# First attention of a two-block forward pass: the first shift from TensorE's matmuls to VectorE's dots, and another order of VectorE's work around the heads

## The chip, the cores and the metric

The kernel runs on one core of one Trainium2 chip. The metric is the device time of one execution in microseconds, as the median of several runs. One launch computes everything in float32. TensorE multiplies weights in two float32r parts each (a high part and the rest), with three matmuls for each product.

## The reference, cut to what matters

Two blocks are computed one after the other on 256 tokens of width 1024. The change touches the very first stage, the multi-head latent attention of layer 0 and what is computed ahead of it:

```
cond = silu(c)                                   # c: 1 x 1024
mod = cond @ ada_w[0] + ada_b[0]                 # 1 x 6144
sh1, sc1, g1, sh2, sc2, g2 = split(mod, 6)
h = rmsnorm(x, norm_g[0, 0]) * (1 + sc1) + sh1   # 256 x 1024
proj = h @ mla_w_in                              # 672 columns: 384 q, 256 kv, 32 rope
c_q, c_kv = rmsnorm(proj[:, :384]), rmsnorm(proj[:, 384:640])
q = c_q @ w_uq; kv = c_kv @ w_ukv                # 16 heads; rope on 32 columns of q and k
o = softmax(q k^T / sqrt(96) + chunk mask) v     # a head at a time
x = x + g1 * (o @ mla_w_out)
h = rmsnorm(x) * (1 + sc2) + sh2
x = x + g2 * (silu(h @ w_gate) * (h @ w_up)) @ w_down
...                                              # a Mamba layer with eight experts, then block two
```

## The kernel before

**Weights.** All weights of the program pass in one list of tiles, in the order in which they are loaded. SyncE loads a tile into the next of six slots of `raw` (`NRAW`) as soon as the tile that was there six places earlier has been used. A tile has one of three kinds.
- "w": ScalarE copies it into `parts` (the high part, `hi`, L245), VectorE subtracts that from it (the rest, `low`, L260), and its slot of `raw` is free after that. `parts` has five places (`NSPLIT`), so tile m's high part waits for the matmuls with tile m - 5. The text counts these tiles as m0, m1 and so on: m0 to m5 are `mla_w_in`, m6 to m17 the up projections of four groups of heads (m6 to m8 for group 0, m9 to m11, m12 to m14 and m15 to m17 for groups 1 to 3), m18 to m25 `mla_w_out`, m26 to m91 the first feed-forward layer in eleven steps (four tiles of gate and up, and two of down, each step), and m92 is the first of the Mamba layer.
- "dot": 128 rows of the transposed `ada_w`. VectorE multiplies it with the broadcast condition row `crow` and sums along the row (L625): 128 of the 6144 numbers of `mod` as a column in `acols`. After each fourth dot the bias is added (L631). `rows_pe` makes a row of four columns with four small matmuls (L292), broadcast over all partitions.
- "plain": TensorE takes it as it is, in float32. Only `Start` uses these.

**Start.** `Start.FIRST = (2, 3, 0, 1)` lists four blocks of 512 columns of `ada_w`: 2 and 3 are `sc1`, 0 and 1 are `sh1`. Each is four plain tiles, eight matmuls (16 instructions in the trace) and a bias matmul. `scale_dve` makes `mod` and the scaled `xn` of each half, and `shift_dve` adds the shift out of the banks. Then TensorE turns `xn` over in four pieces (`x_pieces`), ScalarE and VectorE split each into `hTh` and `hTl` (L414, L421), and the projection `in` begins (L286 to L288).

**Heads.** A slot h of the loop does, on TensorE, the scores of head h, the turning of head h - 1's probabilities and the values of head h - 2. VectorE takes the maximum of head h (L808, L809), the reciprocal of head h - 1 (L842) and the values of head h - 2 (L866). ScalarE does the exponentials (L817, L818). Four slots lie between one group's projections and the next. Among them stand the next group's `kv` and `q` projections, the rotation of its queries (`q_dve`, L1014 to L1029) and the copies of its keys (`kT_dve`, L1074). `K.W.low(v)` stands at written places in `Mla.dve`. It runs all dots that precede the next "w" tile in the list, and then that tile's split.

All orders are written out by hand; each engine runs its own list, and semaphores are waited for where a value comes from another engine. `Ffn.dve` is not changed by the diff: it calls `K.W.low(v, 4)`, then `hid_dve` (the product with silu and its split, L1448 and L1451, between ScalarE's L1439 and L1441), then `K.W.low(v, 2)`, for each step.

## Time and profile before

| what | value |
|---|---|
| median of 3 runs | 2807.74 us (2806.32 to 2808.96) |
| the profiled execution | 2809.04 us, of which 2807.2 us span |
| TensorE matmuls busy | 94% of the span |
| VectorE, ScalarE busy | 70%, 56% |
| DMA | 616.35 MB, mean 220 GB/s |
| granted clock of TensorE, mean | 0.966 |

The profile is of one execution, 1.3 us longer than the median of the runs. Times within it are microseconds from the start of its span. The attention of layer 0 with what precedes it fills about the first 213 us, the first feed-forward layer runs to about 422 us. "Busy" of TensorE says that a matmul was under way, whatever clock it ran at; the clock stands in a column of its own (1.00 is 2.4 GHz, 0.50 is 1.2 GHz).

### The profile page before, as it was taken

The numbers are of one execution on the slowest core, as the hardware profiler recorded it, in microseconds if no ns is written. First come the engines' busy times: TensorE is split into PE (matmuls) and PEld (weight loads), VectorE is DVE, ScalarE is ACT, GpSimd is POOL, SyncE is SP. The second block draws the span as 40 slices with busy tenths as digits, with TensorE's granted clock in tenths as the row PEclk, the third lists the DMA queues.
The fourth block names the chain that finished last, engine by engine and source line by source line (L and its number), as shares of the span: only waits on it lengthen the run. The fifth ranks groups of instructions, "written<-read, shape, count | busy, mean of one in ns | idle before, by whom it ended". The sixth has DMA issues, their size and how long they took to land.

```text
span 2807.2 us, 39117 instructions
## 1 busy us (share of the span) xinstructions
PE 2649.9 (94%) x15496; PEld 2304.3 (82%) x15496; DVE 1961.1 (70%) x2819; ACT 1565.7 (56%) x2266; POOL 10.9 (0%) x24
## 2 busy tenths in 40 slices
PE   7788998998999999999996999999999999999998
PEld 3677998886888888888885998887898998887898
DVE  3768887876898899889896556555555556655555
ACT  2443445653777777778775445465444445455444
POOL 0000000000000000000000000000000000000000
PEclk9889998998999999999997999999999999999999
DMA  8537984514899999999995665434565665434563
GB/s 276 188 119 261 352 311 127 174 48 133 298 365 342 334 350 350 332 344 366 335 354 189 194 185 175 141 98 128 173 188 151 202 185 176 147 97 130 164 186 115
DMA packets 349599, 616.35 MB, mean 220 GB/s; under 512 B 20705, under 2 KB 174881, under 8 KB 349409
## 3 DMA queue, kind: packets, MB, share of 16 engines
q1 hardware_dynamic: 346402, 603.35, 64.6%
q0 software_dynamic: 1872, 5.99, 0.7%
q10 hardware_dynamic: 1136, 4.44, 0.4%
q8 instruction: 125, 2.05, 0.3%
q14 instruction: 64, 0.52, 0.1%
HBM read 612.66 MB, written 1.05 MB: 219 GB/s over the span
## 4 chain that ended last, share of the span: by engine, by line
PE 84%; DVE 8%; ACT 4%; DMA 2%; issue 1%; DVEq 0%; ACTq 0%
PE pb L286 24%; PE pb L288 24%; PE pb L287 24%; PE pb L292 8%; DVE parts L260 2%; PE pb L408 2%; ACT parts L245 1%; DMA raw<-in_moe_w_up 1%; PE pb L2215 1%; PE pb L2671 1%; DVE raw L625 1%; DMA X<-in_x 0%; DVE hTl L421 0%; ACT pb L478 0%; DVE xn L509 0%
## 5 line engine op out<-in xcount | busy, mean ns | idle before, releaser
L260 DVE TENSOR_TENSOR parts<-raw,parts 128x1024 fp32r<-128x1024 f32 (+2 forms) x1051 | 1265.2, 1216 | 590.6 <-ACT parts L245 556.2
L245 ACT ACTIVATE parts<-raw 128x1024 fp32r<-128x1024 f32 (+2 forms) x1051 | 1103.1, 1054 | 824.6 <-PE pb L288 699.7
L286 PE MATMUL pb<-parts,arenar 128*128 128x512 f32 (+2 forms) x1696 | 667.9, 394 | 14.7 <-DVE arenar L421 6.1
L287 PE MATMUL pb<-parts,arenar 128*128 128x512 f32 (+2 forms) x1696 | 649.5, 383 | 0.0
L288 PE MATMUL pb<-parts,arenar 128*128 128x512 f32 (+2 forms) x1696 | 648.7, 382 | 0.0
L286 PE MATMUL pb<-hTh,parts 128*128 128x256 f32 x1952 | 559.5, 287 | 7.3 <-DVE hTl L421 4.9
L287 PE MATMUL pb<-hTl,parts 128*128 128x256 f32 x1952 | 558.3, 286 | 0.0
L288 PE MATMUL pb<-hTh,parts 128*128 128x256 f32 x1952 | 557.9, 286 | 0.0
L286 PEld LDWEIGHTS pb<-hTh,parts 128*128 128x128 f32 x1952 | 381.0, 195 | 11.9 <-issue 7.1
L286 PEld LDWEIGHTS pb<-parts,arenar 128*128 128x128 f32 x1696 | 321.4, 190 | 80.5 <-issue 16.3
L287 PEld LDWEIGHTS pb<-hTl,parts 128*128 128x128 f32 x1952 | 380.9, 195 | 1.8
L288 PEld LDWEIGHTS pb<-hTh,parts 128*128 128x128 f32 x1952 | 380.7, 195 | 0.0
L288 PEld LDWEIGHTS pb<-parts,arenar 128*128 128x128 f32 x1696 | 321.0, 189 | 62.8
L287 PEld LDWEIGHTS pb<-parts,arenar 128*128 128x128 f32 x1696 | 321.5, 190 | 61.3 <-issue 5.6
L286 PE MATMUL pb<-parts,hTh 128*128 128x512 f32 (+3 forms) x560 | 224.2, 400 | 10.9 <-DVE hTl L421 8.4
L288 PE MATMUL pb<-parts,hTl 128*128 128x512 f32 (+3 forms) x560 | 216.5, 387 | 0.0
L287 PE MATMUL pb<-parts,hTh 128*128 128x512 f32 (+3 forms) x560 | 216.2, 386 | 0.0
L286 PEld LDWEIGHTS pb<-parts,hTh 128*128 128x128 f32 x560 | 108.4, 194 | 32.5 <-issue 10.6
L292 PE MATMUL pb<-arena 64*128 64x128 f32 (+6 forms) x696 | 129.6, 319 | 4.7 <-DVE arena L2139 2.6
L288 PEld LDWEIGHTS pb<-parts,hTl 128*128 128x128 f32 x560 | 108.3, 193 | 21.5
L287 PEld LDWEIGHTS pb<-parts,hTh 128*128 128x128 f32 x560 | 108.5, 194 | 17.8
L292 PEld LDWEIGHTS pb<-arena 64*128 64x128 f32 (+3 forms) x696 | 92.6, 195 | 26.1 <-issue 11.8
(287 smaller groups left out, 1969.4 us busy)
## 6 DMA issues: line engine op xcount, KB each, us to landing
raw<-in_moe_w_gate SPq DMA_DIRECT2D x176, 512.0 KB, 5.2
raw<-in_moe_w_up SPq DMA_DIRECT2D x176, 512.0 KB, 5.3
raw<-in_moe_w_down SPq DMA_DIRECT2D x176, 512.0 KB, 5.3
raw<-in_ffn_wg SPq DMA_DIRECT2D x88, 512.0 KB, 4.3
raw<-in_ffn_wu SPq DMA_DIRECT2D x88, 512.0 KB, 3.7
raw<-in_ffn_wd SPq DMA_DIRECT2D x88, 512.0 KB, 4.4
raw<-in_ada_wT SPq DMA_DIRECT2D x80, 512.0 KB, 5.2
raw<-in_w_in SPq DMA_DIRECT2D x72, 512.0 KB, 3.7
```

The lines of the kernel that those rows point to most:

```text
L245: a.e.activation(self.part(t, 0), self.slot(t), ACT.Copy).then_inc(*a.up(self.c.hi, t.m))
L260: v.e.tensor_tensor(self.part(t, 1), self.slot(t), self.part(t, 0).bitcast(F32), ALU.subtract).then_inc(*v.up(self.c.lo, t.m))
L286: e.matmul(o, a[0], b[0], start=start, stop=False, skip_group_check=True)
L287: e.matmul(o, a[0], b[1], start=False, stop=False, skip_group_check=True)
L288: return e.matmul(o, a[1], b[0], start=False, stop=stop, skip_group_check=True)
L292: return e.matmul(o, a, b, start=start, stop=stop, skip_group_check=True)
L408: m = t.e.transpose(b.t[0:w, j * P:(j + 1) * P], s, self.C["ident"])
L625: v.e.scalar_tensor_tensor(out=w, in0=w, scalar=1.0, in1=self.crow, op0=ALU.mult, op1=ALU.mult, accum_out=self.acols[:, o:o + 1]).then_inc ...
L2215: m = t.e.transpose(b.t[:, k * P:(k + 1) * P], self.hc[:, i % 2, k * P:(k + 1) * P], self.K.C["ident"])
L2671: m = t.e.matmul(b.t[:, 0:2 * NCMP], loads[k // 8][:, k % 8, :], self.flat[:, a, k, :], start=k == 0, stop=k == 15)
```

## The change

Six things are edited; all else is as it was.
- `FIRST` is `(2, 3)`. The shift's two blocks are no longer matmuls of plain tiles but eight dot tiles, `dot_tiles(0)` and `dot_tiles(1)`. Four of them stand among the scale's eight plain tiles (two plain, one dot, and so on), four behind. TensorE makes the rows out of the columns with four small matmuls each.
- `scale_dve` takes one half at a time, and dots stand ahead of each half and behind both.
- `low` counts "w" tiles and dots apart (`n_lo`, `n_dot`), and `dots` can be called alone.
- A slot of a head takes the maximum and the reciprocal first, then `low` (the dots and the split), then the values. `q_dve` and `kT_dve` stand behind the third slot instead of ahead of it.
- Within group 0, the rope of the keys and the turning of `krT` stand ahead of `q_dve` and `kv_pe`. Both pieces of `c` are turned before `q_pe`. No dot stands there but one. ScalarE's high parts of m9 to m13 are made together or later.
- The table of dots ahead of each tile is spread from m4 on instead of m4 to m7 and m13 on.

```diff
     def low(self, v, times=1):
-        while times and self.n_low < len(self.tiles):
-            t = self.tiles[self.n_low]
-            self.n_low += 1
-            if t.kind == "dot":
-                v.wait_ge(*self.landed(t))
-                self.dot(v, t, self.slot(t))
-            if t.kind != "w":
-                continue
-            times -= 1
+        for t in self.cut[self.n_lo:self.n_lo + times]:
+            while self.n_dot < len(self.dotted) and self.dotted[self.n_dot].n < t.n:
+                self.dots(v)
+            assert all(x.n > t.n - self.nraw for x in self.dotted[self.n_dot:]), t.label
             self.n_lo += 1
...
+    def dots(self, v, times=1):
+        for t in self.dotted[self.n_dot:self.n_dot + times]:
+            self.n_dot += 1
+            v.wait_ge(*self.landed(t))
+            self.dot(v, t, self.slot(t))
...
-    FIRST = (2, 3, 0, 1)
+    FIRST = (2, 3)
...
+        scale = [Tile(("ada", n, k0), w[:, k0:k0 + 2, n * 512:n * 512 + 512], (2, 512), "plain")
+                 for n in self.FIRST for k0 in (0, 2, 4, 6)]
+        shift = self.K.dot_tiles(0)
+        mixed = sum(([*scale[2 * i:2 * i + 2], shift[i]] for i in range(4)), [])
+        return mixed + self.K.dot_tiles(1)
...
+        for n in range(2):
+            b = K.c.bk[4 + n]
+            t.wait_ge(*K.c.dv.val(("col", n)))
+            t.wait_ge(*b.turn(("ada", n)))
+            for j in range(4):
+                m = mm1(t.e, b.t[:, j * P:(j + 1) * P], K.acols[:, 4 * n + j:4 * n + j + 1].to_broadcast([P, P]),
+                        K.C["ident"])
+            m.then_inc(*t.up(K.c.pe, ("ada", n)))
...
-        dots = {4: 1, 5: 1, 6: 1, 7: 1, 22: 1, 23: 1} | {m: 2 for m in range(13, 22)}
+        dots = {m: 1 for m in (4, 5, 6, 7, 8, 9, 10, 12, 13, 14)} | {m: 2 for m in range(15, 22)}
...
     def slot_dve(self, v, h, lows=0):
         if h < 16:
             self.att.max_dve(v, h)
         if 1 <= h <= 16:
             self.att.sums_dve(v, h - 1)
+        self.K.W.low(v, lows)
         if h >= 2:
             self.att.values_dve(v, h - 2)
...
         self.c_pe(t, 0)
+        self.c_pe(t, 4)
         self.q_pe(t, 0)
-        self.c_pe(t, 4)
-        self.kv_pe(t, 0)
-        b = c.bk[6]
         t.wait_ge(*c.dv.val("kr"))
         K.turn_pe(t, "krT", 6, [self.kr[:, tt, :] for tt in range(2)])
+        self.kv_pe(t, 0)
...
         for j in range(2):
             self.qT_act(a, 0, j)
+        K.W.hi(a, 4)
...
-        self.start.scale_dve(v)
+        K.W.dots(v, 2)
+        self.start.scale_dve(v, 0)
+        K.W.dots(v, 2)
+        self.start.scale_dve(v, 1)
+        K.W.dots(v, 4)
+        K.W.low(v)
         self.start.shift_dve(v)
-        K.W.low(v, NSPLIT - 2)
-        for key, b, tt, k0, hi, lo in self.x_pieces():
+        for i, (key, b, tt, k0, hi, lo) in enumerate(self.x_pieces()):
             K.parts_dve(v, key, b, hi, lo)
+            if i % 2:
+                K.W.low(v)
...
         for g in range(1, 4):
             h = 4 * g - 4
-            K.W.low(v)
-            self.slot_dve(v, h)
-            K.W.low(v)
-            self.slot_dve(v, h + 1)
-            K.W.low(v)
+            for s in range(3):
+                self.slot_dve(v, h + s, 1)
             self.q_dve(v, g)
             for j in range(2):
                 self.kT_dve(v, g, j)
-            self.slot_dve(v, h + 2)
             self.slot_dve(v, h + 3)
```

On VectorE, at the start of the program, ahead of the first split pieces of `hT`, the order before was this (the `scale` operations write `mod` and `xn`, the `shift` operations read a bank `pb`):

```order
L744 SCALAR_TENSOR_TENSOR mod<-pb,grow 128x512 [waits s_matmul_done]
L748 SCALAR_TENSOR_TENSOR xn<-X,small,mod 128x512 [waits s_bank7_out]
L748 SCALAR_TENSOR_TENSOR xn<-X,small,mod 128x512
L762 TENSOR_TENSOR xn<-xn,pb 128x512 [waits s_matmul_done,s_vector_done]
L762 TENSOR_TENSOR xn<-xn,pb 128x512 [waits s_vector_done]
L762 TENSOR_TENSOR xn<-xn,pb 128x512 [waits s_matmul_done]
L762 TENSOR_TENSOR xn<-xn,pb 128x512 [waits s_vector_done]
L260 TENSOR_TENSOR parts<-raw,parts 128x1024 [waits s_weight_hi] x3
L421 TENSOR_TENSOR hTl<-pb,hTh 128x4x128 [waits s_scalar_done] x4
```

The change has this at the same place, from the second half of the scale on:

```order
L758 SCALAR_TENSOR_TENSOR mod<-pb,grow 128x512 [waits s_matmul_done]
L762 SCALAR_TENSOR_TENSOR xn<-X,small,mod 128x512 [waits s_bank7_out]
L762 SCALAR_TENSOR_TENSOR xn<-X,small,mod 128x512
L628 SCALAR_TENSOR_TENSOR raw,small<-raw,arena 128x1024 [waits s_raw0_landed]
L628 SCALAR_TENSOR_TENSOR raw,small<-raw,arena 128x1024 [waits s_raw1_landed]
L628 SCALAR_TENSOR_TENSOR raw,small<-raw,arena 128x1024 [waits s_raw2_landed]
L628 SCALAR_TENSOR_TENSOR raw,small<-raw,arena 128x1024 [waits s_raw3_landed]
L634 TENSOR_TENSOR small<-small 128x4 [waits s_vector_done]
L256 TENSOR_TENSOR parts<-raw,parts 128x1024 [waits s_weight_hi]
L776 TENSOR_TENSOR xn<-xn,pb 128x512 [waits s_matmul_done,s_weight_lo]
L776 TENSOR_TENSOR xn<-xn,pb 128x512 [waits s_vector_done]
L776 TENSOR_TENSOR xn<-xn,pb 128x512 [waits s_matmul_done]
```

Four dots and one split have come between the scale and the shift, and two of the three splits that stood ahead of the pieces of `hT` have gone among them. Four more dots stand further up.

On VectorE, around the third slot of the second group of heads, the order before was this (dots L625, split L260, then `q_dve` and `kT_dve`, then the slot's maximum):

```order
L625 SCALAR_TENSOR_TENSOR raw,small<-raw,arena 128x1024 [waits s_raw3_landed]
L625 SCALAR_TENSOR_TENSOR raw,small<-raw,arena 128x1024 [waits s_raw4_landed]
L260 TENSOR_TENSOR parts<-raw,parts 128x1024 [waits s_weight_hi]
L1014 TENSOR_SCALAR arena<-pb,small 128x384 [waits s_matmul_done] x2
...
L1074 COPY arena<-pb 64x512 [waits s_matmul_done] x2
L808 TENSOR_REDUCE small<-pb 128x1 [waits s_matmul_done]
L809 TENSOR_REDUCE small<-pb 128x1
L842 RECIPROCAL small<-small 128x2 [waits s_bank6_out,s_bank4_out]
L866 TENSOR_SCALAR arena<-pb,small 128x64 [waits s_vector_done,s_matmul_done]
```

The change has there:

```order
L822 TENSOR_REDUCE small<-pb 128x1 [waits s_matmul_done]
L823 TENSOR_REDUCE small<-pb 128x1
L856 RECIPROCAL small<-small 128x2 [waits s_bank6_out,s_bank4_out]
L628 SCALAR_TENSOR_TENSOR raw,small<-raw,arena 128x1024 [waits s_raw2_landed]
L628 SCALAR_TENSOR_TENSOR raw,small<-raw,arena 128x1024 [waits s_raw3_landed]
L256 TENSOR_TENSOR parts<-raw,parts 128x1024 [waits s_weight_hi]
L880 TENSOR_SCALAR arena<-pb,small 128x64 [waits s_weight_lo,s_matmul_done]
L880 TENSOR_SCALAR arena<-pb,small 128x64
L1028 TENSOR_SCALAR arena<-pb,small 128x384 x2
```

The maximum and the reciprocal of the third slot now precede the dots, the split and `q_dve`.

On VectorE, at the end of the first feed-forward layer's normalisation (the last two pieces of `hT`, then the splits of its weights, then dots), before:

```order
L421 TENSOR_TENSOR hTl<-pb,hTh 128x4x128 [waits s_scalar_done]
L260 TENSOR_TENSOR parts<-raw,parts 128x1024 [waits s_weight_hi] x3
L625 SCALAR_TENSOR_TENSOR raw,small<-raw,arena 128x1024 [waits s_raw4_landed]
L625 SCALAR_TENSOR_TENSOR raw,small<-raw,arena 128x1024 [waits s_raw5_landed]
L625 SCALAR_TENSOR_TENSOR raw,small<-raw,arena 128x1024 [waits s_raw0_landed]
```

and now:

```order
L424 TENSOR_TENSOR hTl<-pb,hTh 128x4x128 [waits s_scalar_done]
L256 TENSOR_TENSOR parts<-raw,parts 128x1024 [waits s_weight_hi] x4
L628 SCALAR_TENSOR_TENSOR raw,small<-raw,arena 128x1024 [waits s_raw4_landed]
L628 SCALAR_TENSOR_TENSOR raw,small<-raw,arena 128x1024 [waits s_raw5_landed]
L628 SCALAR_TENSOR_TENSOR raw,small<-raw,arena 128x1024 [waits s_raw0_landed]
```

The calls of `low` in the attention split 27 tiles before and split 26 now, so VectorE makes one split more here, and stays one tile further back in the list, against its other work, until the experts' last steps. ScalarE's high parts are as far along as they were.

## Rows read from the trace of the kernel before

**Rows 1.** The page: busy us, share of the span and instructions of each engine.
```profile
PE 2649.9 (94%) x15496; PEld 2304.3 (82%) x15496; DVE 1961.1 (70%) x2819; ACT 1565.7 (56%) x2266; POOL 10.9 (0%) x24
```

**Rows 2.** Stretches: us, busy PE, PEld, DVE, ACT, POOL; clock, DMA share, GB/s.
```profile
25.60:50.00 24.40, 24.40 (x56) 9.78 (x55) 5.59 (x8) 3.17 (x3) 0.00 (x0) 1.00 0.80 258
56.30:61.20 4.90, 4.85 (x12) 3.82 (x13) 4.90 (x7) 0.00 (x0) 0.00 (x0) 0.50 0.68 192
61.20:75.00 13.80, 13.80 (x86) 12.31 (x85) 7.46 (x13) 4.83 (x13) 0.00 (x0) 0.99 0.81 278
79.40:85.40 6.00, 6.00 (x20) 5.91 (x20) 2.23 (x12) 2.75 (x7) 0.00 (x0) 0.51 0.32 125
114.80:120.70 5.90, 0.01 (x2) 0.01 (x1) 5.66 (x18) 0.91 (x4) 0.00 (x0) 0.60 0.66 237
```

**Rows 3.** Timeline of TensorE: start, us, operation, count, [idle before, and its releaser].
```profile
33.74 7.13 PE L292 MATMUL pb<-raw,small 128*128 128x512 f32 x16
...
56.35 0.77 PE L286 MATMUL pb<-parts,hTh 128*128 128x512 f32 x1 [4.15 <-DVE hTl L421]
...
79.39 0.66 PE L286 MATMUL pb<-parts,arenar 128*128 128x384 f32 x1 [3.32 <-DVE arenar L421]
...
97.21 0.66 PE L408 MATMUL pb<-cst,small 128*96 128x128 f32 x2 [4.23 <-DVE small L1346]
97.66 3.62 PE L408 MATMUL pb<-cst,arena 128*96 128x128 f32 x16
...
128.08 0.83 PE L292 MATMUL pb<-arena 96*128 96x128 f32 x6
...
151.92 0.83 PE L292 MATMUL pb<-arena 96*128 96x128 f32 x6
...
173.17 1.48 PE L292 MATMUL pb<-arena 96*128 96x128 f32 x6
```

**Rows 4.** Timeline of VectorE up to the first weights.
```profile
23.48 0.18 DVE L1332 TENSOR_SCALAR small<-small 128x32 f32<-128x32 f32 x1
...
50.08 1.41 DVE L762 TENSOR_TENSOR xn<-xn,pb 128x512 f32<-128x512 f32 x2 [6.64 <-PE pb L292]
51.41 3.49 DVE L260 TENSOR_TENSOR parts<-raw,parts 128x1024 fp32r<-128x1024 f32 x3
54.81 2.47 DVE L421 TENSOR_TENSOR hTl<-pb,hTh 128x512 fp32r<-128x512 f32 x4
...
58.34 1.21 DVE L625 SCALAR_TENSOR_TENSOR raw<-raw,arena 128x1024 f32<-128x1024 f32 x1
```

**Rows 5.** DMA of 0 to 60 us: GB/s in 40 slices; loads, median to landing.
```profile
GB/s 0 172 204 362 401 394 355 133 268 393 411 407 400 412 388 350 270 350 247 190 220 272 300 335 137 292 224 221 298 299 213 188 337 330 294 75 301 179 282 45
...
raw<-in_ada_w SPq DMA_DIRECT2D x16, 512.0 KB, 4.7
```

**Rows 6.** Timeline of VectorE between the projection and the heads of group 1.
```profile
97.91 2.29 DVE L1268 COPY arena<-pb 32x2048 f32<-32x2048 f32 x1 [0.75 <-PE pb L408]
...
101.32 0.68 DVE L1074 COPY arena<-pb 64x512 f32<-64x512 f32 x1 [0.17 <-PE pb L408]
...
138.94 1.13 DVE L1014 TENSOR_SCALAR arena<-pb,small 128x384 f32<-128x384 f32 x2
```

**Rows 7.** Waits between 100 and 175 us: total us, times, longest.
```profile
PE pb L408 <- ACT arena L818: 19.0, 6, 6.2
```

**Rows 8.** The first feed-forward layer and the Mamba layer's start: a stretch, and timelines.
```profile
300.00:350.00 50.00, 50.00 (x354) 47.13 (x354) 43.88 (x64) 23.28 (x32) 0.00 (x0) 1.00 0.96 349
...
198.49 1.23 DVE L260 TENSOR_TENSOR parts<-raw,parts 128x1024 fp32r<-128x1024 f32 x1
...
225.75 3.49 DVE L260 TENSOR_TENSOR parts<-raw,parts 128x1024 fp32r<-128x1024 f32 x3
...
280.38 0.42 DVE L1448 TENSOR_TENSOR arena<-arena,pb 128x256 f32<-128x256 f32 x1
...
440.82 0.55 PE L286 MATMUL pb<-hTh,parts 128*128 128x256 f32 x1 [1.72 <-DVE hTl L421]
```

More of the change, by code:

```diff
@@ L199, in __init__ @@
         self.cut = [t for t in tiles if t.kind == "w"]
+        self.dotted = [t for t in tiles if t.kind == "dot"]
         self.place = {t.label: n for n, t in enumerate(tiles)}
@@ L677, in tiles @@
         w = wview(self.K.A["ada_w"][0])
-        return [Tile(("ada", n, k0), w[:, k0:k0 + 2, n * 512:n * 512 + 512], (2, 512), "plain")
-                for n in self.FIRST for k0 in (0, 2, 4, 6)]
+        scale = [Tile(("ada", n, k0), w[:, k0:k0 + 2, n * 512:n * 512 + 512], (2, 512), "plain")
[3 more added lines that the diff above has]
+        return mixed + self.K.dot_tiles(1)
     def sp(self, s):
@@ L735, in dve, with scale_dve @@
             K.stats_dve(v, "n0", tt)
[L737 removed]
+    def scale_dve(self, v, h):
         K, c, dv = self.K, self.K.c, self.K.c.dv
         v.wait_ge(*K.row_landed(0))
[L741 to L749 removed]
+        b, cs = c.bk[6 + h], slice(h * 512, (h + 1) * 512)
+        v.wait_ge(*c.pe.val(("ada", 2 + h)))
+        v.e.scalar_tensor_tensor(out=K.mod[:, 1, cs], in0=b.t[:, :], scalar=1.0, in1=K.row(0)[:, cs], op0=ALU.add,
+                                 op1=ALU.mult).then_inc(*v.up(b.out, ("ada", 2 + h)))
+        v.wait_ge(*v.tail)
+        for tt in range(2):
+            v.e.scalar_tensor_tensor(out=K.xn[:, tt, cs], in0=K.X[:, tt, cs], scalar=K.rst[:, tt:tt + 1],
+                                     in1=K.mod[:, 1, cs], op0=ALU.mult, op1=ALU.mult).then_inc(*v.up(dv))
     def shift_dve(self, v):
@@ L1236, in act @@
             self.slot_act(a, h + 2)
+            K.W.hi(a)
             self.slot_act(a, h + 3)
@@ L1256, in dve @@
         self.in_dve(v, 0)
-        K.W.low(v, 2)
+        self.in_dve(v, 1)
+        K.W.dots(v)
         self.c_dve(v, 0)
-        self.in_dve(v, 1)
+        self.c_dve(v, 4)
         self.roots_dve(v)
-        K.W.low(v, 2)
-        self.c_dve(v, 4)
+        self.key_rope_dve(v)
         self.q_dve(v, 0)
-        K.W.low(v)
-        self.key_rope_dve(v)
         b = c.bk[6]
```

24 lines of the change are left out of this document (6 added, 18 removed).

## The prediction

> **What bounds the kernel now.** I read the page first: TensorE is busy 94% of the span, VectorE 70% [rows 1]. That mean hides the stage which is changed. Its stretches come next [rows 2]. From 25.6 to 50 us TensorE is busy without a pause, while VectorE has 5.6 us of work in 24.4. From 114.8 to 120.7 it is the other way round: VectorE 5.7 of 5.9 us, TensorE 0.01. So the scale and shift matmuls bound the first 50 us, and VectorE bounds much of the head loop. TensorE's timeline [rows 3] shows where it stands before a dependent start: 4.15 us before the projection at 56.35 (for `hTl`), 3.32 us before the queries at 79.39, 4.23 us before the key turning at 97.21. In the head loop it waits 19.0 us in six waits for exponentials [rows 7]. These are not late for ScalarE's sake but because the maximum ahead of them is queued behind VectorE's dots, split and `q_dve`.
>
> All that follows the attention starts from its end, so a shift there passes through to the end of the program, less what VectorE's new place in the weight list costs later.
>
> **1. The front, up to the projection.** A block of plain matmuls takes 7.13 us and its bias about 1 us [rows 3]; two go, 16 us. In their place stand eight dots of 1.14 us each (1.21 in the row, which overlaps its neighbour) [rows 4]: 9.2 us. The loads stay 16 tiles of 512 KB ahead of m0. Nothing moves faster than about 400 GB/s, 1.3 us a tile, and a tile lands 4.7 us after its issue [rows 5]. I walk the new list with these.
> - The first six loads do not wait, as before, and block 2 ends at 25.6. VectorE is free at 23.7 [rows 4]: dots 0 and 1 end at 24.8 and 26.0. The third dot's load and all behind it now wait for dot 0, and land at about 29, 30.4, 31.7 and 33. Block 3 has two plain tiles of these and ends at 35 instead of 33.8.
> - The second half of the scale (2.1 us) ends at 37.3. The last four dots, landed by 38.3, end at 41.9, and the column's bias at 42.1. Split m0 ends at 43.3 (the tile lands at about 39.4, where the list before had it at 44.5). The shift, twice 1.4 us, ends at 46.1, and the first two pieces of `hTl` at 47.4.
>
> The projection starts at 47.4 instead of 56.35: **-8.9**. Before, from the shift's end at 51.5 three splits (3.4 us) preceded the pieces [rows 4]; now one does, and one is hidden among them. If the loads came no faster than at the 258 GB/s of that stretch [rows 2], m2 would land 3 to 4 us later and ScalarE's pieces, queued behind its high part, with it: -5.
>
> **2. From the projection to the first keys.** It took 45.6 us from 56.35 to the second key copy's end at 102.0 [rows 3, 6]. Now: the projection runs 18.6 us as before, to 66.0, cold at its start as before. `in_dve(1)` and one dot end at 67.9, the two turned pieces of `c` at 69.2 and 69.6. The queries' matmuls start at 69.2 (3.3 us behind the projection instead of 4.4) and take 6 us at half clock. The roots and key rope, 4.2 us, run on VectorE beside them, where before they came later and behind two splits and two dots. So `krT` and `kv` follow at once: TensorE reaches 80.1, turns queries and keys (3.6 us [rows 3]) to 83.8; the copy of 2.29 us [rows 6] and split m9 lie beside that, and the second key copy ends at 84.5. That is 37.1 us: **-8.5**. What was skipped must now be made before the first maximum: `low(3)` is two dots and three splits, 4.9 us, where two dots and a short split stood, 3.9 us. Further, ScalarE's high part of m13 waits for a tile loaded into a slot that a dot frees at 85.6, and ends at 90, just when the maximum is ready; the table load of the exponential is hidden in it. I take **+1.0** for both, bounds 0 and +4 (a load at 4.7 us and one load queued ahead of it).
>
> **3. The head loop.** Dots fall from six to four in the first group: two times 1.14, of which the walk keeps **-1.6** at the next group's first scores (head 4, ending at 110.9 instead of 128.9 [rows 3], with all terms so far). For the second group I add VectorE's work from scores to rope: maximum, reciprocal, two dots, split, values are 4.3, 4.0 and 4.6 us, two waits of 0.5 for scores, and 2.8 for `q_dve` (138.94 on, [rows 6]). Then follow on TensorE 1.8 us of turning, 4.0 of the next `kv` at partly half clock and 1.0 of scores: 23.5 against 23.8 before (to 152.75). The third group gives 21.4 against 21.9 (to 174.65 [rows 3]). So **-0.8** for both. The stall is moved, not removed: the exponential no longer waits behind `q_dve`, but `q_dve` and with it the next group's queries wait behind the third slot's dots and split. The tail from head 12 on is TensorE's and stays.
>
> Attention: -8.9 - 8.5 + 1.0 - 1.6 - 0.8 = **-18.8**.
>
> **4. The clock, a gain not in the sum above.** From 79.4 to 85.4 TensorE ran at 0.51 after 3.32 us idle [rows 2, 3]. Now it idles some 2 us there. If it stays at full speed, 3 us of 6 go, of which the rope lets 2.8 through. Taken at a quarter: **-0.7**. The Trainium skill (TensorE: Matmul & The Clock Gate, What's actually happening) has the clock follow recent activity, full after sustained work and half after idleness. By it the bursts between waits stay half-speed, and the term would be 0; the rows show both levels, 0.50 at 56.3 and 0.99 from 61.2.
>
> **5. VectorE one tile further back.** One fewer `low` in the attention has three prices.
> - The feed-forward layer's first tile was split at 198.49, under TensorE's matmuls; three splits stood ahead of the dots at 225.75 [rows 8]. Now four do, and one slot of six stays filled, so one more load of 1.3 us lies between there and m30, for which TensorE waits at 240: **+1.3**.
> - In each step `hid_dve` moves ahead of a dot and a split. VectorE stands for a silu which ScalarE makes behind the next tile's high part: 2 tiles of 1.3 us, 0.4 for silu, less the split of 1.2, 1.8 us a step. A step is 120 matmuls, 354 take 50 us, so 16.95 us [rows 8]. VectorE is busy 43.88 of 50 us, 14.9 a step, 15.2 with the gaps in `hid_dve` (280.38 to 282.87). With the new wait it needs 17.0 to 17.1, just above TensorE. Besides, the slots of two tiles come free some 4 us later, with DMA busy 0.96 of the stretch; the round of load, high part and silu grows by up to 1.1 us. Bounds: 0 (TensorE stays the bound) and 1.1 over nine steps, 10. I take 0.4: **+3.5**. By the Trainium skill (DMA: Bandwidth & Descriptors, Where 436 GB/s comes from) some 358 GB/s is what memory gives a core; the row's 349 is close, and by that rule a hole is not made up, which is the upper bound.
> - The Mamba layer's first tile was split ahead, and TensorE began at 440.82 when `hTl` was there [rows 8]. Now the split comes between: **+0.8**. Some **+0.4** for two or three places in Mamba and the experts, by the same shift; bounds 0 and 1.5.
>
> **The sum.** -18.8 - 0.7 + 1.3 + 3.5 + 0.8 + 0.4 = -13.5. It is made against the profiled execution, 2809.04 to 2795.5; that one lies 1.3 over the median, so the median goes from 2807.74 to **2794.2**.
>
> **Rivals.**
> - *A. As summed*, with the feed-forward stage giving back a third: -9 to -17, 2791 to 2799. Chance 0.50.
> - *B. TensorE stays the bound of the feed-forward steps*, and the clock helps. For it speaks that TensorE is busy 50.00 of 50, and a tile's lead there may take 2 us. Then -18.8 - 2.1 + 1.3 + 0.8 + 0.4 = -18.4: 2789 (2784 to 2791). Chance 0.20.
> - *C. The later silu bites fully*, 1.1 in nine steps, or the head groups lose what they win since `q_dve` waits behind 3.4 us of dots and split, 2 us a group. DMA share 0.96 speaks for the first, VectorE's 5.66 of 5.9 for the second. -13.5 + 6 = -7.5: 2800 (2799 to 2802). Chance 0.18.
> - *D. The front gives little*: the interleaved loads wait for VectorE, and 0.8 of DMA is busy [rows 2] already. Front -4 instead of -8.9, and some of C: -4, 2804. Chance 0.07; it is "no change" when under 5.6 us.
> - *E. Slower.* One mechanism: the silu wait in the feed-forward layer also idles DMA, so each of eleven steps grows. It decides from 18 / 11 = 1.6 us a step on, half of a split and dot more than I can find; at 2.5 us it gives -17 + 27 = +10, 2818. Against it: two splits and two dots' worth of wait a step would have to be paid in full. Chance 0.05.
>
> 0.2% is 5.6 us, about what a measurement of this kernel can tell from no change. Faster: A, B, C and none of D, 0.88. Same 0.07, slower 0.05. The range 2787 to 2802 takes A, C and half of B.
>
> **What would show it.** In the trace after: the projection's first matmul at 47 to 48; the second key copy ending at 82 to 85; scores of head 4 near 111, of head 8 near 134.5, of head 12 near 156; four splits in a row 18 to 20 us earlier than 225.75; steps of the feed-forward layer at 17.0 (B), 17.3 (A) or 18 us (C); TensorE's start in Mamba 0.8 us behind `hTl`. I am wrong if the third dot's load is later than 26, if `krT` still waits for the key rope, or if high part m13 holds the first exponential beyond 93.

## The result and the profile after

| | median us | lowest to highest | runs |
|---|---|---|---|
| before | 2805.99 | 2801.73 to 2808.97 | 10 |
| after | 2812.74 | 2808.86 to 2820.73 | 10 |

The ratio is 1.0031, with a 95% interval of 1.0020 to 1.0043: the change makes the kernel slower by 0.3%, where 0.5% faster was forecast. The profiled execution of after, 2808.86 us with a span of 2807.1, is the fastest of its ten, and that of before, 2809.04 us, is longer than any of its ten, so the two traces show less of the difference than the medians do.

The page after, in the form of [rows 1], shows hardly anything:

```profile
PE 2637.7 (94%) x15476; PEld 2300.9 (82%) x15476; DVE 1963.3 (70%) x2837; ACT 1565.1 (56%) x2266; POOL 10.9 (0%) x24
```

What tells is when TensorE first uses a weight tile. This table is read from the traces of before, of after, and of two experiments below (e1: after, with VectorE's missing split made up at the attention's end; e2: before, with that split taken out). Shifts are against before, in us.

| tile | before at | after | e1 | e2 |
|---|---|---|---|---|
| m0, projection | 56.35 | -8.95 | -8.76 | +0.08 |
| m1 | 61.50 | -11.18 | -10.98 | -0.15 |
| m9, keys of group 1 | 101.29 | -20.29 | -20.41 | -0.31 |
| m18, output projection | 181.18 | -20.74 | -20.47 | -0.42 |
| m25, its last | 207.39 | -20.74 | -20.46 | -0.41 |
| m26, feed-forward layer | 224.70 | -18.42 | -20.46 | +1.91 |
| m50 | 300.06 | -12.55 | -21.02 | +7.52 |
| m86, its last step | 401.94 | -1.24 | -20.84 | +19.39 |
| m92, Mamba layer | 440.82 | +3.14 | -18.28 | +23.57 |
| m550, late in the experts | 1311.86 | +3.98 | -22.16 | +25.67 |

The attention won 20.7 us, and by m92 all of it was given back: 2.3 us at m26, 17.2 from there to m86, 3.4 from m86 to m88 and 1.0 at m92. The first part lies at TensorE's start in the layer. The wait for VectorE at m26, then at m30, was this before:

```profile
224.70 0.55 PE L286 MATMUL pb<-hTh,parts 128*128 128x256 f32 x1 [0.22 <-DVE hTl L421]
...
240.00 0.39 PE L286 MATMUL pb<-hTh,parts 128*128 128x256 f32 x1 [1.83 <-DVE parts L260]
```

and is this after, where m26's own split is late and m30's less so:

```profile
206.28 0.58 PE L289 MATMUL pb<-hTh,parts 128*128 128x256 f32 x1 [2.54 <-DVE parts L256]
...
221.12 0.39 PE L289 MATMUL pb<-hTh,parts 128*128 128x256 f32 x1 [0.81 <-DVE parts L256]
```

The 3.4 us between m86 and m88 are 0.9 us of wait and 2.5 us of clock in the 48 matmuls of the rows. These three lines are of before, of after and of e1; the granted clock over them was 1.00, 0.64 and 0.63:

```profile
410.66 5.97 PE L292 MATMUL pb<-cst,small 128*128 128x128 f32 x48 [2.80 <-DVE arena L1448]
```

```profile
410.31 8.44 PE L295 MATMUL pb<-cst,small 128*128 128x128 f32 x48 [3.69 <-DVE arena L1464]
```

```profile
389.82 8.54 PE L295 MATMUL pb<-cst,small 128*128 128x128 f32 x48 [2.80 <-DVE arena L1464]
```

e1 has no lag and the wait of before, and its trace lost the 2.5 us as well, so they don't come of the lag.

**The attention after.** TensorE's timeline (start, us, operation, count, idle before and its releaser), at the places of [rows 3]:

```profile
68.57 0.66 PE L289 MATMUL pb<-parts,arenar 128*128 128x384 f32 x1 [2.47 <-DVE arenar L424]
...
73.85 0.42 PE L411 MATMUL pb<-cst,small 128*96 128x128 f32 x2 [0.54 <-DVE small L1362]
...
106.96 0.83 PE L295 MATMUL pb<-arena 96*128 96x128 f32 x6
...
130.25 0.83 PE L295 MATMUL pb<-arena 96*128 96x128 f32 x6
...
152.37 1.48 PE L295 MATMUL pb<-arena 96*128 96x128 f32 x6
```

The key turning at 73.85 waits 0.54 us for the rope, where it waited 4.23. Heads 4, 8 and 12 are scored 21.1, 21.7 and 20.8 us sooner than in [rows 3]. VectorE's two key copies, in the form of [rows 6], and the wait of [rows 7], 20 us sooner (80 to 155 us), which was 19.0 us in six:

```profile
80.17 1.28 DVE L1088 COPY arena<-pb 64x512 f32<-64x512 f32 x2
```

```profile
PE pb L411 <- DVE arena L1043: 4.8, 3, 1.9
PE pb L295 <- DVE arena L880: 4.7, 5, 2.7
PE pb L411 <- ACT arena L832: 4.2, 2, 2.6
```

The stall is in good part moved. TensorE is spared 14.8 us of waits for exponentials (L832), and waits 9.5 us for the rotated queries (L1043) and for VectorE's values (L880).

**The feed-forward layer after.** The same stretch as in [rows 8] (us, busy PE, PEld, DVE, ACT, POOL; clock, DMA share, GB/s), and the waits in it (total us, times, longest):

```profile
300.00:350.00 50.00, 45.89 (x332) 43.23 (x331) 39.53 (x58) 21.11 (x29) 0.00 (x0) 1.00 0.85 304
```

```profile
DVE arena L1464 <- ACT arena L1455: 5.0, 3, 1.9
...
PE pb L289 <- DVE parts L256: 4.1, 3, 1.9
```

TensorE, busy for all of 50 us before, now waits 4.1 us, each time for a split. VectorE is idle too: in each step it waits for the silu. Nobody is the bound of this stretch by busy time. One round through SyncE (SPq), ScalarE, VectorE and TensorE, step m54 to m59 and the next, reads:

```profile
301.08 0.42 DVE L1464 TENSOR_TENSOR arena<-arena,pb 128x256 f32<-128x256 f32 x1 [1.56 <-ACT arena L1455]
...
303.57 1.22 DVE L628 SCALAR_TENSOR_TENSOR raw<-raw,arena 128x1024 f32<-128x1024 f32 x1
...
304.71 1.22 DVE L256 TENSOR_TENSOR parts<-raw,parts 128x1024 fp32r<-128x1024 f32 x1
...
309.27 2.36 DVE L256 TENSOR_TENSOR parts<-raw,parts 128x1024 fp32r<-128x1024 f32 x2
...
320.27 0.42 DVE L1464 TENSOR_TENSOR arena<-arena,pb 128x256 f32<-128x256 f32 x1 [1.53 <-ACT arena L1455]
```

```profile
311.66 0.38 SPq L237 DMA_DIRECT2D raw<-in_ffn_w_up  x1
```

```profile
318.91 1.06 ACT L246 ACTIVATE parts<-raw 128x1024 fp32r<-128x1024 f32 x1 [1.43 <-DMA raw<-in_ffn_w_up]
319.87 0.37 ACT L1455 ACTIVATE arena<-pb 128x256 f32<-128x256 f32 x1
```

```profile
305.99 0.39 PE L289 MATMUL pb<-hTh,parts 128*128 128x256 f32 x1 [1.25 <-DVE parts L256]
325.18 0.39 PE L289 MATMUL pb<-hTh,parts 128*128 128x256 f32 x1 [1.95 <-DVE parts L256]
```

From `hid_dve` to `hid_dve` it is a closed loop: `hid_dve` 2.49 us (301.08 to 303.57); dots and splits until m59's split frees a slot of `raw`, 8.06 (303.57 to 311.63); the load of the up tile m62 is issued 0.03 later, at 311.66, and its high part can begin 7.25 us later; 0.96 more until the silu, which ScalarE's list has behind that high part; 0.40 until `hid_dve`. The sum, 19.19 us, is the distance of the two TensorE starts (325.18 - 305.99 = 19.19). While VectorE stands for the silu and makes `hid_dve` it frees no slot, and the loads run dry. DMA of 300 to 320 us, in 40 slices of 0.5 us:

```profile
GB/s 381 395 408 457 418 410 328 205 41 0 0 106 131 311 410 197 188 311 303 246 274 350 344 367 360 350 373 379 432 393 381 375 389 412 444 399 369 383 418 428
```

### The profile page after: what moved, and what is told of

Its sections match the earlier page's. It is cut to its first block, busy times and chain, and to the rows that moved or that the text cites. A ratio compares the mean times of both kernels' runs of the same rounds, so it can differ in the third digit from the quotient of the medians.

```text
span 2807.1 us, 39082 instructions
## 1 busy us (share of the span) xinstructions
PE 2637.7 (94%) x15476; PEld 2300.9 (82%) x15476; DVE 1963.3 (70%) x2837; ACT 1565.1 (56%) x2266; POOL 10.9 (0%) x24
## 4 chain that ended last, share of the span: by engine, by line
PE 73%; DVE 13%; DMA 7%; ACT 5%; issue 2%; DVEq 0%; ACTq 0%
PE pb L289 21%; PE pb L291 21%; PE pb L290 21%; PE pb L295 8%; DVE parts L256 5%; DMA raw<-in_moe_w_gate 2%; DVE raw L628 2%; DMA raw<-in_ffn_w_up 2%; PE pb L411 2%; ACT parts L246 2%; DMA raw<-in_moe_w_up 1%; PE pb L2687 1%; PE pb L2231 1%; DMA X<-in_x 0%; DVE hTl L424 0%
## 5 line engine op out<-in xcount | busy, mean ns | idle before, releaser
L289 PE MATMUL pb<-hTh,parts 128*128 128x256 f32 x1952 | 561.4, 288 | 20.2 <-DVE parts L256 17.2
L290 PEld LDWEIGHTS pb<-parts,hTh 128*128 128x128 f32 x560 | 107.1, 191 | 17.5
```

What stands on the lines that cost most here:

```text
L289: e.matmul(o, a[0], b[0], start=start, stop=False, skip_group_check=True)
L290: e.matmul(o, a[0], b[1], start=False, stop=False, skip_group_check=True)
```

## The experiments

Times are compared through the ratio to the kernel before, run on the same chip.

| | edit | median us | ratio | 95% interval | step m50 to m86 |
|---|---|---|---|---|---|
| before | | | | | 16.98 |
| after | | 2812.74 | 1.0031 | 1.0020 to 1.0043 | 18.87 |
| e1 | after, lag made up | 2783.24 | 0.9929 | 0.9912 to 0.9946 | 17.01 |
| e2 | before, lag alone | 2833.16 | 1.0101 | 1.0085 to 1.0116 | 18.96 |
| e3 | after, ScalarE back too | 2784.88 | 0.9925 | 0.9905 to 0.9945 | 17.18 |
| e4 | after, short dots | 2804.22 | 1.0000 | 0.9988 to 1.0012 | 17.86 |
| e5 | after, short loads | 2793.00 | 0.9969 | 0.9959 to 0.9979 | 16.98 |
| e6 | after, silu sooner | 2791.37 | 0.9966 | 0.9954 to 0.9979 | 16.98 |
| e7 | e1, heads as before | 2783.55 | 0.9934 | 0.9922 to 0.9946 | 16.98 |
| e8 | after, keys as before | 2794.98 | 0.9973 | 0.9963 to 0.9982 | 16.98 |
| e9 | e1, silu and `hid_dve` sooner | 2781.68 | 0.9920 | 0.9907 to 0.9933 | 17.15 |
| e10 | e9, heads as before | 2783.90 | 0.9928 | 0.9914 to 0.9941 | 16.98 |
| e11 | e9, in both such layers | 2782.53 | 0.9920 | 0.9902 to 0.9938 | 17.05 |
| e12 | e6, lag made up later | 2787.18 | 0.9937 | 0.9922 to 0.9951 | 16.98 |

The last column is the distance of TensorE's starts of m50 and m86, over six steps.

### e1 and e2: the lag, away and alone

```diff
 # e1, on after, Mla.dve
             self.O_dve(v, tt, 4)
-        K.W.low(v)
+        K.W.low(v, 2)
         K.rows_dve(v, 0, 0, 2, (5, 6))
 # e2, on before, the same place
             self.O_dve(v, tt, 4)
-        K.W.low(v)
         K.rows_dve(v, 0, 0, 2, (5, 6))
```

> The changed kernel with one split more on VectorE at the attention's end (it makes m26 and m27 there, so that from the feed-forward layer on VectorE stands where it stood before the change). Theory L (the lag): all that the attention won, 20.7 us at the first tile of the output projection, was given back in the feed-forward layer because hid_dve had moved one tile forward against the splits; then the steps fall back to 16.98 us, and the time is 18 to 22 us under that of before, about 2786 us. Rival T (the time itself): the feed-forward layer starts 20 us earlier and meets the DMA queue in another phase, so that its steps lengthen whatever VectorE's place; then the steps stay at 18.5 to 19 us and the time stays within 5 us of that of the changed kernel, about 2810 us.

> The kernel before with the split at the attention's end taken out: nothing of the change but its lag of one tile. Theory L: the attention stays as before, each of the feed-forward layer's steps from the second on takes 18.5 to 19 us instead of 16.98, some 18 to 21 us in all, with 3 to 5 us more in the starts and the experts: 22 to 27 us slower than before, about 2830 us. Rival T: the lag by itself costs no more than the prediction had for it, 6 us: about 2812 us.

Theory L held both ways. e1 keeps the 20.5 us through the feed-forward layer (the table of tiles), with TensorE busy throughout:

```profile
300.00:350.00 50.00, 50.00 (x354) 47.12 (x354) 42.60 (x65) 22.57 (x30) 0.00 (x0) 1.00 0.95 342
```

e2 has nothing of the change but the lag, and loses 19.4 us by m86 and 23.6 by m92. In it VectorE waits for the silu as in after, and TensorE for the split:

```profile
DVE arena L1447 <- ACT arena L1438: 4.8, 3, 1.6
```

```profile
325.81 0.39 PE L286 MATMUL pb<-hTh,parts 128*128 128x256 f32 x1 [1.00 <-DVE parts L260]
```

By the ratios the lag costs 1.0% in either kernel: 1.0101 - 1 alone, 1.0031 - 0.9929 within the change, 28 us. In the traces 21.4 us of them are there at m92 (+3.14 against -18.28). The rival, that an earlier start of the layer lengthens its steps, is out: e1 starts 20 us earlier with steps of 17.0.

### e3 and e4: the silu's place, or VectorE's load

```diff
 # e3, on after, Mla.act, at its end
         for tt in range(2):
             self.O_act(a, tt, 4)
-        K.W.hi(a)
 # e4, on after, dot_dve
+        crow = self.crow
+        if 40 <= o < 96:
+            w, crow = w[:, 0:64], crow[:, 0:64]
```

> The changed kernel with ScalarE's high part at the attention's end (m26) taken out, so that ScalarE too stands one tile further back and makes each silu behind the high part of the second gate tile instead of behind that of the first up tile. Theory S (a closed round: the slot of an up tile comes free, its load lands 7 us later, its high part, the silu queued behind it, hid_dve, then dots and splits that free the next slots): the silu leaves the round, VectorE's waits of 1.5 to 1.9 us a step for it go, and the steps return to 17.0 to 17.3 us: 15 to 20 us under the time of before in the feed-forward layer, less 1 to 3 us at the starts, about 2790 us. Rival V (the 2.5 us of hid_dve and the dot ahead of the first up tile's split are enough by themselves, since the split had 2.9 us of slack): the waits for the silu go, but the steps stay at 18 us or more; about 2803 us or more.

> The changed kernel; the 56 dots of the feed-forward layer's list multiply only 64 of the 1024 columns (the rest of these dots is left out; loads are as they were), so that VectorE has 5 times 1.1 us less in a step. Theory S (closed round): the round of 19.2 us has three or four dots of 1.14 us in it, so it falls to about 15 us, below TensorE's 16.98; steps of 17.0 us, time about 2787 us. Rival D (loads set the step: too few slots in flight whatever VectorE does): the steps stay near 18.5 us and the time within 6 us of the changed kernel's.

In e3 VectorE lags as in after, yet the waits for the silu are gone and TensorE waits 0.7 us in 50:

```profile
300.00:350.00 50.00, 49.28 (x347) 46.20 (x346) 42.59 (x63) 21.74 (x29) 0.00 (x0) 1.00 0.95 344
```

So `hid_dve` and a dot ahead of the split don't cost by themselves what the silu's wait costs; rival V falls. The lag stays everywhere in e3, at m92 too (2.74 us of wait for the split), and yet it is as fast as e1. e3 came out 5 us better than expected: by m133 its shift is -23.4. Two of TensorE's waits in the Mamba layer, 1.9 and 0.9 us in e1, are 0.4 and none there.

In e4 neither expectation came true. With VectorE busy 26.8 us of 50 instead of 39.5 the step fell only to 17.86, not to 17.0, and the time to 2804, not to 2787:

```profile
300.00:350.00 50.00, 47.23 (x325) 43.75 (x324) 26.82 (x60) 20.13 (x25) 0.00 (x0) 1.00 0.88 310
```

```profile
DVE arena L1467 <- ACT arena L1458: 4.7, 2, 3.1
```

```profile
raw<-in_ffn_w_up SPq DMA_DIRECT2D x6, 512.0 KB, 7.5
```

Slots come free sooner after `hid_dve`, but then their loads share DMA and land after 7.5 us (6.6 in after's same stretch). My expectation had subtracted the dots from the round and held the landing fixed. Rival D, steps that stay near 18.5, doesn't fit either: the dots are a part of the round, the smaller one.

### e5 and e6: the loads, and the silu in this layer alone

```diff
 # e5, on after, dots: the whole slot is multiplied, as in after
-            self.dot(v, t, self.slot(t))
+            self.dot(v, t, self.raw[:, t.n % self.nraw, 0:1024])
 # and dot_tiles: 64 of 1024 columns are loaded
+        w = 64 if 10 <= n < 24 else D
-        return [Tile(..., self.A["ada_wT"][(4 * n + j) * P:(4 * n + j + 1) * P, :], (D,), "dot")
+        return [Tile(..., self.A["ada_wT"][(4 * n + j) * P:(4 * n + j + 1) * P, 0:w], (w,), "dot")
 # e6, on after, Ffn.act
-            K.W.hi(a, 4)
+            K.W.hi(a, 3 if self.first else 4)
             self.hid_act(a, j)
+            K.W.hi(a, 1 if self.first else 0)
```

> The changed kernel; the 56 dots of the feed-forward layer's list load only 64 of their 1024 columns and multiply the whole slot as before (the other columns are what the slot held, so these dots are not those of the reference), so that VectorE and the order are as in the changed kernel and DMA has 5 x 492 KB less in a step. With the dots shortened instead of their loads (e4) the steps stayed at 17.1 to 18.9 us, so VectorE's own work is little of the round. Theory S with loads in the round (the silu waits behind a high part whose load was issued only when hid_dve had let the splits free a slot, and which then lands 7 us later because six loads share DMA): landing falls from 7 to about 4 us, the round from 19.2 to 16 us, and TensorE's 16.98 sets the step: about 2788 us. Rival V (VectorE's row of hid_dve, dots and splits sets the step): steps stay at 18 us or more, about 2805 us or more.

> The changed kernel; in the first feed-forward layer alone ScalarE makes the silu of a step after three high parts instead of after four, then the fourth. VectorE keeps its lag everywhere, ScalarE's place outside this layer is as in the changed kernel. Theory S: the silu's place behind the late high part is the whole cause in that layer, so its steps fall to about 17.0 us and the time to within 4 us of the version that catches up at the attention's end (2783.2), less the 3 to 4 us which the lag costs in the starts and experts: 2784 to 2790 us. Rival O (moving ScalarE back helped in e3 for another reason: its place in the Mamba layer and the experts, where e3 won 5 us more): the feed-forward steps stay over 18 us and the time stays over 2800 us.

In e5 nothing is changed on the engines, the silu's wait is still there, and TensorE doesn't notice: the up tile lands after 4.7 us instead of 6.6.

```profile
300.00:350.00 50.00, 50.00 (x354) 47.13 (x353) 42.13 (x64) 22.27 (x30) 0.00 (x0) 1.00 0.67 198
```

```profile
DVE arena L1465 <- ACT arena L1456: 4.8, 3, 1.9
```

```profile
raw<-in_ffn_w_up SPq DMA_DIRECT2D x6, 512.0 KB, 4.7
```

One round of e5, walked in the same way from `hid_dve` at 307.12 to the next at 323.88, is 2.48 + 8.26 + 0.03 + 4.63 + 0.96 + 0.40 = 16.76 us. The one term that differs from the 19.19 of after is the landing, 4.63 for 7.25:

```profile
307.12 0.42 DVE L1465 TENSOR_TENSOR arena<-arena,pb 128x256 f32<-128x256 f32 x1 [1.89 <-ACT arena L1456]
...
323.88 0.42 DVE L1465 TENSOR_TENSOR arena<-arena,pb 128x256 f32<-128x256 f32 x1 [1.44 <-ACT arena L1456]
```

```profile
317.89 0.38 SPq L237 DMA_DIRECT2D raw<-in_ffn_w_up  x1
```

```profile
322.52 1.06 ACT L246 ACTIVATE parts<-raw 128x1024 fp32r<-128x1024 f32 x1 [1.33 <-DMA raw<-in_ffn_w_up]
```

So the landing time is what carries the round above TensorE's 16.98. The time of e5, 2793.0 us, is 5 us over the expected 2788, though its steps are as expected; it keeps the lag outside this layer, as e6 does. In e6 loads and dots are whole, and ScalarE makes the silu behind the second gate tile's high part (which begins at 307.11):

```profile
307.11 1.06 ACT L246 ACTIVATE parts<-raw 128x1024 fp32r<-128x1024 f32 x1 [1.59 <-DMA raw<-in_ffn_w_gate]
308.07 0.36 ACT L1455 ACTIVATE arena<-pb 128x256 f32<-128x256 f32 x1
```

```profile
308.20 1.23 DVE L256 TENSOR_TENSOR parts<-raw,parts 128x1024 fp32r<-128x1024 f32 x1 [0.29 <-ACT parts L246]
309.35 0.41 DVE L1464 TENSOR_TENSOR arena<-arena,pb 128x256 f32<-128x256 f32 x1
```

```profile
300.00:350.00 50.00, 50.00 (x354) 47.12 (x354) 43.73 (x66) 23.48 (x31) 0.00 (x0) 1.00 0.98 351
```

The silu is ready while VectorE still splits, VectorE doesn't wait for it, and the step is 16.98 with the lag in place (2791.4 us, just over the 2784 to 2790 expected). That fixes the cause in this layer: not the lag itself but that it puts `hid_dve` ahead of the up tile's split while ScalarE still makes the silu behind that tile's high part.

### e12: the rest of the lag

```diff
 # on e6, Ffn.dve, behind the last step
+        if self.first:
+            K.W.low(v)
```

> As e6 (the changed kernel, silu one tile sooner on ScalarE in the first feed-forward layer), and VectorE makes one split more at that layer's end, so that from the Mamba layer on it stands as in e1. e6 came out at 0.9966 of before, e1 at 0.9929, 10 us apart, of which their traces show 1.0 us as a wait (TensorE's start in the Mamba layer, 2.74 against 1.72 us) and the rest as stretches at a lower granted clock. Theory L2: the lag costs in the Mamba layer and the experts too, more than that wait, so the time falls to that of e1, 2780 to 2785 us. Rival C: the rest is the clock's own variation and only the wait goes, 1 to 2 us: 2789 to 2791 us.

e6 and e12 differ by 0.29% (8 us by the ratios, 4.2 by the medians). Their intervals lie only just apart (0.9954 to 0.9979, and 0.9922 to 0.9951), so the size is loose, and e12's 2787.2 us falls between the two expectations (2780 to 2785 and 2789 to 2791). One microsecond of it shows: TensorE's start in the Mamba layer, in e6 and then in e12.

```profile
422.01 0.55 PE L289 MATMUL pb<-hTh,parts 128*128 128x256 f32 x1 [2.74 <-DVE parts L256]
```

```profile
422.51 0.55 PE L289 MATMUL pb<-hTh,parts 128*128 128x256 f32 x1 [1.72 <-DVE hTl L424]
```

At m550 the two traces stand 0.3 us apart. So the timed runs lean to theory L2, that the lag costs outside the layer too, but don't settle it: where the other microseconds lie is not shown and stays open. Nor is it the lag alone, since e3 keeps it everywhere, with ScalarE one tile back as well, at 0.9925. A pair of traces can't well be asked for them because of the clock. e1 and e6 at the Mamba layer, from m93 to m100, the same matmuls:

```profile
427.30:451.41 24.11, 24.11 (x194) 24.11 (x193) 15.09 (x24) 14.29 (x25) 0.00 (x0) 0.93 0.64 191
```

```profile
427.18:454.50 27.32, 27.32 (x195) 27.32 (x193) 14.80 (x25) 14.29 (x25) 0.00 (x0) 0.81 0.52 162
```

That is 3.2 us by the granted clock alone (0.93 against 0.81). Without a lag it occurs as well: e7's took 27.26.

### e7, e8, e10: what each part of the attention is worth

```diff
 # e7, on e1, Mla.dve (and Mla.act in the order of before)
-            for s in range(3):
-                self.slot_dve(v, h + s, 1)
+            K.W.low(v)
+            self.slot_dve(v, h)
+            K.W.low(v)
+            self.slot_dve(v, h + 1)
+            K.W.low(v)
             self.q_dve(v, g)
 ...
+            self.slot_dve(v, h + 2)
             self.slot_dve(v, h + 3)
 # e8, on after: Mla.pe, Mla.act and Mla.dve between in_dve(0) and kT_dve as before, five splits there
```

> The version that catches up (e1, 2783.2 us) with the head loop's order of before on VectorE and ScalarE (dots and split ahead of each slot, q_dve ahead of the third slot's maximum); front and key part stay changed. The prediction's term for the head loop is -2.4 us: about 2785.5 us, with head waits for exponentials near 19 us again. Rival: the shift from m9 to m18 between the two traces is only -0.4 us, so the order is worth nothing: 2783 us. A third: the order is needed since the dots have been spread (m8 to m14), and is worth more than 5 us.

> The changed kernel with the part from the projection to the first keys as it was before (order of TensorE, ScalarE and VectorE, and its five splits there, so VectorE has no lag later); front and head loop stay changed. The prediction's terms for this part are -8.5 and +1.0; the two traces show -9 us from m1 to m9. So it should be 7 to 9 us slower than the version that catches up (2783.2): 2790 to 2792 us. Rival: the head loop takes back what the keys win, since VectorE's dots bound it: under 3 us, 2786 us or less.

> As e9, with the head loop's order of before on VectorE and ScalarE, on the same chip as e9: e7 against e1 left open whether the new order is worth 2.6 us (the shift at m18 in their traces) or nothing (their medians). Theory: 2 to 4 us over e9. Rival: within 1.5 us of e9.

Head loop: m18 is used at 163.31 in e7 and 160.71 in e1 (2.6 us), at 162.95 in e10 and 161.54 in e9 (1.4 us); the ratios differ by 0.0005 and 0.0008, within their intervals. The traces bear out 1 to 3 us; the medians can't tell it from nothing. These pairs compare the two orders with the dots spread as in the change; they don't price the change of the loop against before.

Keys: m18 in e8 is 13.0 us later than in e1, and the time 0.44% more (12 us). That is more than forecast, since the old order doesn't even keep what the new front won. TensorE's timeline of e8:

```profile
73.15 0.66 PE L289 MATMUL pb<-parts,arenar 128*128 128x384 f32 x1 [6.34 <-DVE arenar L424]
```

Ahead of the queries TensorE stands 6.34 us instead of 3.32 [rows 3]: two dots and two splits, with a wait for a high part, lie ahead of the turned `c`. With 0.61 and 2.47 us there in the changed kernel, taking dots and splits out of this piece is the likely worth of the key part. e8 puts the place of the key rope and ScalarE's order back too, so the parts aren't told apart.

### e9 and e11: a version that beats both

```diff
 # e9, on e1, Ffn.act and Ffn.dve alike (low for hi)
-            K.W.hi(a, 4)
+            K.W.hi(a, 3 if self.first else 4)
             self.hid_act(a, j)
+            K.W.hi(a, 1 if self.first else 0)
```

> The version that catches up at the attention's end (e1), and in the first feed-forward layer both ScalarE's silu and VectorE's hid_dve stand one tile sooner (after three high parts and three splits of a step instead of four). Theory: the steps are TensorE's at 16.98 us in both, so nothing is won there; the last step and the rows behind it (m86 to m88) took 17.0 us in e1 and 12.6 us in e6, where the silu was one tile sooner, so 2 to 4 us are won at the layer's end: 2779 to 2781 us by e1's 2783.2 (ratio to before 0.991 to 0.9925). Rival: hid_dve ahead of the first up tile's split makes that split late for TensorE as in the changed kernel, since the split had 2.6 us of slack and hid_dve with a dot takes 3.6: steps over 17.5 us and a time over 2790 us.

> As e9, with silu and hid_dve one tile sooner in the second feed-forward layer too. That layer has no dots in its list, so its loads have room; expected within 3 us of e9. Rival: hid_dve ahead of the split delays TensorE there by over 1 us a step: over 10 us more than e9.

e9 is 0.8% faster than before (2781.68 us, 0.9907 to 0.9933), and 1.1% faster than the changed kernel. Against e1 it isn't told apart: at the layer's end m86 to m88 takes 13.4 us instead of 17.0, as expected, though only 1.3 us of that are TensorE's wait ahead of the rows (1.2 and 0.3 us for 2.8) and 2.3 are the clock in them (the granted clock was 1.00 in e9 and 0.63 in e1). But e9 stood 2.5 us behind e1 at m86, 0.8 of it from the attention and most of the rest from two longer steps (17.8 us from m44 to m50, 17.9 to m56). e11 is the same within the intervals. e1, one number in one line, has nearly all of it.

## Why the prediction was wrong

By its own steps:

- **1, the front, -8.9: right.** The projection starts at 47.40, 8.95 us sooner. But "cold at its start as before" was wrong, and in the good sense: m1 is used 2.2 us sooner still. From 47.40 to 52.50 the granted clock was 0.98, where it had been 0.50 in the projection's first 4.9 us [rows 2], since TensorE had turned `xn` until just before (from 43.83 on, without a pause) instead of standing for 4.15 us.

```profile
47.40:52.50 5.10, 5.10 (x23) 4.25 (x23) 5.10 (x6) 2.91 (x4) 0.00 (x0) 0.98 0.38 80
```

- **2, projection to first keys, -8.5 and +1.0: right, a little small.** The key copies end at 81.45, 3 us before the 84.5 of the walk, 2.2 of them from the warm projection.
- **3, the head loop, -1.6 and -0.8: the first right, the second not.** With the +1.0 ahead of it the first was to bring -0.6 from the key copies to head 4, and the traces have -0.6 (-20.55 to -21.12). From head 4 to head 12 they have +0.3 (-21.12 to -20.80) where -0.8 was summed. The stall is moved, as the prediction said, and more of it is left than it summed.
- Together the attention was to win 18.8 us, 19.5 with the clock, and won 20.7. That this is so close is in part luck: up to the key copies the clock gave more than its term, and the head loop gave less than its own.
- **4, the clock, -0.7: the mechanism was there, and larger.** It paid 2.2 us in the projection, where the term had nothing. In its own place it paid 1.2: the queries' eighteen matmuls took 4.7 us (68.57 to 73.31) instead of 5.9 (79.39 to 85.28), since the granted clock, 0.50 up to 70 us, was 1.00 from 72 on. The Trainium skill (TensorE: Matmul & The Clock Gate, What's actually happening) has the clock follow recent activity, and these rows fit that; my use of it, that bursts between waits stay half-speed and the term would be 0, did not: the queries' burst began at half clock and ended at full.
- **5, VectorE one tile further back: this is the step that failed.** Its first price, +1.3, was nearly right in size (1.9 by m30) and wrong in its mechanism: the wait at m30, which a further load was to lengthen, fell from 1.83 to 0.81 us, and TensorE waited 2.54 us for m26's own split instead of 0.22. Its third, +0.8 at the Mamba layer, measured 1.0 (the wait grew from 1.72 to 2.74). Its second, "I take 0.4: +3.5", with bounds of 0 and 1.1 a step, measured 1.9 a step: 11.3 us from m50 to m86. Against e1 the changed kernel stood 19.6 us behind at m86, of which 2.0 were there at m26: 17.6 us for a term of 3.5.

Where inside that step? Its pieces were sound: it had VectorE standing for the silu for 1.8 us, and the rows have 1.5 to 1.9; it named the two slots that come free later. Then it compared *rates*: VectorE's work with its waits, 17.0 to 17.1 a step, against TensorE's 16.98, and bounded the rest by 1.1. But VectorE, ScalarE and the loads were no longer three engines side by side. The lag had linked them into one loop, and a loop's period is the sum of its latencies, whatever share each engine is busy. With the numbers of before it was there to be added up: `hid_dve` 2.5, seven dots and splits to the freeing one 8.1, landing 5.5 to 6 (medians of 300 to 350 us), high part and silu 1.4, together 17.5 to 18.0 us, over TensorE's 16.98 by 0.5 to 1.0. That alone would have stayed within the prediction's bound of 1.1. What carried the step past it is that the landing is not constant: after the hole six loads are issued 1.1 us apart (305.96 to 311.66), faster than the 1.3 us in which the prediction had DMA move one, and the last of them landed after 7.25 us.

The holes themselves are made up in part: the slices above run between 344 and 444 GB/s in the last 9.5 us, 387 in the mean, and yet the stretch has 304 instead of 349 [rows 8]. The prediction took 358 GB/s from the Trainium skill (DMA: Bandwidth & Descriptors, Where 436 GB/s comes from) as what memory gives a core, by which nothing would be made up; the slices go above that, so the measurement decides. The Trainium skill (HBM Reference, Specifications (TRN2)) gives about 425 GB/s for a core that streams alone, as this one does, and the mean of 387 lies under that.

**The rivals.** E, "the silu wait in the feed-forward layer also idles DMA, so each of eleven steps grows", is what happened, at the place named, and beyond the point from which it was to decide (1.6 us a step; 1.9 measured). It had a chance of 0.05. What spoke against it, "two splits and two dots' worth of wait a step would have to be paid in full", was again an argument on work, not on the loop. A, B and C all rested on bounds for that term which didn't hold it, so the range of 2787 to 2802 had no room for the result. Without the lag the forecast would have been -18.8 - 0.7 = -19.5, and e1 gives -20 (0.71% of 2806).

## What to carry to other kernels

- When an edit changes how many of one kind of step an engine has made, count the total and carry the offset through the whole program: here one split fewer in the attention cost 28 us, some 20 of them in a layer that the diff never touches, and one more call in the attention gave it back.
- Where an engine's wait is for something queued behind a load, and the load waits for a slot which that engine frees, don't compare busy shares. Walk the loop once and add its latencies; if the sum is above the step, every step pays the difference, and a shallow ring of slots gives nothing to hide it in.
- A wait that recurs each step with a hole in the DMA slices beside it was the mark of such a loop here. It was cut at the item that was out of place (the silu, one position sooner in ScalarE's list), not by taking work off the engine that looks busy (e4).

## What the runs showed of the hardware

- Landing time depends on how loads bunch: the same 512 KB up tile landed after 6.0 us before (median of its six in the stretch), 6.6 after, 7.5 with shorter dots, and 4.7 with the neighbouring loads cut to 32 KB. Shortening VectorE's work lengthened it.
- One kernel's executions differ in the granted clock. Over the span it was 0.964 or 0.965 in the four longest of after's ten (2815.13 to 2820.73 us) and 0.966 to 0.968 in the others (2808.86 to 2812.80). Two traces show where such a difference can lie. The small row matmuls behind the experts, both behind a wait of 0.78 us, had a granted clock of 0.59 in the trace of before and 1.00 in that of after (first before, then after):

```profile
1504.88 1.79 PE L292 MATMUL pb<-arena 128*128 128x512 f32 x2 [0.78 <-DVE arena L2139]
```

```profile
1510.21 1.12 PE L295 MATMUL pb<-arena 128*128 128x512 f32 x2 [0.78 <-DVE arena L2155]
```

  From there to the start of the next layer this trace of before lost 2.6 us to that of after. The +5.3 us which after had lost by then (m675) are -0.2 at the trace's end; half of that is this stretch, most of the other half goes between 1757 and 1773 us, where the granted clock is 0.79 before and 1.00 after. The medians, 6.8 us apart, don't share it. The Trainium skill (TensorE: Matmul & The Clock Gate, What's actually happening) calls the number of cold matmuls variable from run to run. These two traces are of two kernels, alike in this stretch, so they fit that without showing it. For a difference under some 5 us, a pair of traces compared at their ends says little; compared tile by tile, with the clock beside each stretch, it says what happened.
